# Eight bonus-sum products moved behind the last head's transposes, and their copy moved between two steps of the block inverses

## The reference

```python
def even_mixer(h, positions, w_in, ...):
    proj = h @ w_in
    a_qkv, b_rkv = proj[..., :3 * WIDTH_A], proj[..., 3 * WIDTH_A:]
    ...
    y_a = dilated_attention(q, k, v).transpose(0, 2, 1, 3).reshape(Bb, S, WIDTH_A)
    y_b = rwkv7_mixer(h, b_rkv, ...)
    return jnp.concatenate([y_a, y_b], axis=-1) @ w_out

def rwkv7_mixer(h, rkv, ...):
    ...
    ys = rwkv7_bidir_scan(both(r_h, 1), orient(heads(decay), 1), orient(k_dir, 1), orient(a_vec, 1), orient(b_vec, 1), both(v_h, 1))
    yf = unorient(ys, 1)
    ...
    bonus = (jnp.sum(r_h * (k_dir[0] + k_dir[1]) * r_k, axis=-1, keepdims=True) * v_h).reshape(Bb, S, WIDTH_B)
    return ((yn + bonus) * gate).astype(h.dtype)
```

## Time and profile before

| what | us |
|---|---|
| median of 3 runs | 1690.72 |
| lowest and highest of them | 1690.38, 1691.57 |
| time of the profiled execution | 1692.2 |
| its span, first to last instruction | 1690.5 |
| PE busy | 1655.8 |
| DVE busy | 1250.9 |
| ACT busy | 988.1 |
| POOL busy | 76.2 |

### The profile page before, as it was taken

One profiled execution on the slowest core, in us unless ns is written; L12 is line 12 of the kernel. 1 busy time (PEld: TensorE's weight loads), 2 busy tenths in 40 slices (PEclk: granted clock), 3 DMA queues, 4 the chain that ended last, 5 costly groups with the idle time before them and its releaser, 6 DMA issues.

```text
span 1690.5 us, 22416 instructions
## 1 busy us (share of the span) xinstructions
PE 1655.8 (98%) x8628; PEld 1370.1 (81%) x8628; DVE 1250.9 (74%) x1197; ACT 988.1 (58%) x958; POOL 76.2 (5%) x95
## 2 busy tenths in 40 slices
PE   7999999999999999899999999999999999999997
PEld 3868995999988885788888888888888888888886
DVE  5578545544423763788988888988888988988886
ACT  2356434443443432677677676776776777777774
POOL 2005230000000030000000000000000000000000
PEclk9999999999999999899999999999999999999999
DMA  6410014555542302899999999999999999999993
GB/s 244 110 70 27 2 51 150 175 177 198 174 150 100 133 18 102 303 368 378 325 366 374 330 366 370 330 365 368 334 364 367 329 366 353 350 366 351 345 378 123
DMA packets 199507, 428.86 MB, mean 254 GB/s; under 512 B 10746, under 2 KB 34574, under 8 KB 199438
## 3 DMA queue, kind: packets, MB, share of 16 engines
q1 hardware_dynamic: 199438, 427.90, 70.2%
HBM read 426.82 MB, written 1.05 MB: 253 GB/s over the span
## 4 chain that ended last, share of the span: by engine, by line
PE 97%; DVE 2%; ACT 1%; DMA 0%; issue 0%; SPq 0%; DVEq 0%; ACTq 0%
PE bank L2677 18%; PE bank L2679 18%; PE bank L2678 18%; PE bank L2457 5%; PE bank L2387 4%; PE bank L2388 4%; PE bank L2386 4%; PE bank L1962 2%; PE bank L1975 2%; PE bank L2152 2%; PE bank L2686 2%; PE bank L2620 2%; PE bank L2356 2%; PE bank L2175 2%; PE bank L2724 1%; PE bank L2538 1%
## 5 line engine op out<-in xcount | busy, mean ns | idle before, releaser
L1900 DVE TENSOR_TENSOR split<-ring,split 128x2048 fp32r<-128x2048 f32 x336 | 764.1, 2290 | 112.8 <-ACT split L1119 109.8
L1119 ACT ACTIVATE split<-ring 128x2048 fp32r<-128x2048 f32 x336 | 640.1, 1924 | 175.4 <-PE bank L2679 173.8
L2677 PE MATMUL bank<-split 128*128 128x512 f32 x896 | 354.6, 396 | 2.7 <-DVE split L1872 1.4
L2679 PE MATMUL bank<-split 128*128 128x512 f32 x896 | 349.8, 390 | 0.0
L2678 PE MATMUL bank<-split 128*128 128x512 f32 x896 | 349.1, 390 | 0.0
L2677 PEld LDWEIGHTS bank<-split 128*128 128x128 f32 x896 | 168.4, 188 | 36.2 <-issue 1.7
L2679 PEld LDWEIGHTS bank<-split 128*128 128x128 f32 x896 | 168.2, 188 | 35.8
L2678 PEld LDWEIGHTS bank<-split 128*128 128x128 f32 x896 | 168.6, 188 | 33.5
L2677 PE MATMUL bank<-split,ehr_ 128*128 128x512 f32 x448 | 180.6, 403 | 1.8 <-DVE ehr_ L1892 1.8
L2679 PE MATMUL bank<-split,ehr_ 128*128 128x512 f32 x448 | 175.6, 392 | 0.0
L2678 PE MATMUL bank<-split,ehr_ 128*128 128x512 f32 x448 | 175.3, 391 | 0.0
(11 more groups left out here) (478 smaller groups left out, 1972.7 us busy)
## 6 DMA issues: line engine op xcount, KB each, us to landing
ring<-in_od_moe_gate SPq DMA_DIRECT2D x112, 1024.0 KB, 6.9
ring<-in_od_moe_up SPq DMA_DIRECT2D x112, 1024.0 KB, 7.3
ring<-in_od_moe_down SPq DMA_DIRECT2D x112, 1024.0 KB, 6.5
ring<-in_od_w_in SPq DMA_DIRECT2D x7, 2048.0 KB, 7.6
ring<-in_ev_w_in SPq DMA_DIRECT2D x6, 2048.0 KB, 9.1
ring<-in_ev_ffn_gate SPq DMA_DIRECT2D x11, 1024.0 KB, 5.3
ring<-in_ev_ffn_up SPq DMA_DIRECT2D x11, 1024.0 KB, 7.9
ring<-in_ev_ffn_down SPq DMA_DIRECT2D x5, 2048.0 KB, 7.8
```

What stands on the lines that cost most here:

```text
L1119: act.activation(wst[:, r % NSTAGE, 0, :], ring[:, (r % NHALF) * HALF:(r % NHALF + 1) * HALF], ACT.Copy).then_inc(w_hi, 1)
L1900: dve.tensor_tensor(wst[:, r % NSTAGE, 1, :], ring[:, (r % NHALF) * HALF:(r % NHALF + 1) * HALF], wst[:, r % NSTAGE, 0, :].bitcast(F32), S ...
L2677: pe.matmul(o, hi, wh, start=start, stop=False)
L2679: return pe.matmul(o, lo, wh, start=False, stop=stop)
```

## The change

The products of token tile 0 stay where they were, behind the transposes of head 6. Those of token tile 1 are issued one step later, behind the transposes of head 7 and ahead of `values(7)`; the count `bon_ps` is raised by the last of them. `bonus_copy` is called inside level 8, behind its first `products`, and no longer ahead of the level.

```diff
@@ block_inverses
                     if b in meanwhile:
                         meanwhile[b]()
                     products(((Bk, b, w), 1, 32), ((Tb, 0, w), 32, 1))
+                    if (b, "products") in meanwhile:
+                        meanwhile[b, "products"]()
                     link(dve.tensor_reduce(strided(Xs, 0, (1, n * b * b)), strided(tmp, 0, (b, n * b * b), (1, b)),
                                            AX.X, ADD))
@@ vector
-            block_inverses(gather_all, {4: lambda: head_scores(7), 8: bonus_copy}, whole(Xm), Tb, whole(Tm), Xs, Tc, Pc).then_inc(dve_step, 1)
+            block_inverses(gather_all, {4: lambda: head_scores(7), (8, "products"): bonus_copy}, whole(Xm), Tb, whole(Tm), Xs, Tc, Pc).then_inc(dve_step, 1)
@@ tensor
-            def bonus_sums():
+            def bonus_sums(a):
                 pe.wait_ge(vt_sb, 2)
                 pe.wait_ge(dve_step, DVE_STEPS["bon_rdy"])
-                for a in range(TT):
-                    for j in range(4):
-                        last = pe.matmul(B[6][:, HA * a:HA * a + HA], bonT[:, SEQ * j + P * a:SEQ * j + P * a + P],
-                                         head_ind[:, j, :], start=(j == 0), stop=(j == 3))
-                last.then_inc(bon_ps, 1)
+                for j in range(4):
+                    last = pe.matmul(B[6][:, HA * a:HA * a + HA], bonT[:, SEQ * j + P * a:SEQ * j + P * a + P],
+                                     head_ind[:, j, :], start=(j == 0), stop=(j == 3))
+                if a == TT - 1:
+                    last.then_inc(bon_ps, 1)
@@
-                elif h == 6:
-                    bonus_sums()
+                elif h >= 6:
+                    bonus_sums(h - 6)
```

## The result

| kernel | runs | lowest | median | highest | above 1695 us |
|---|---|---|---|---|---|
| before | 22 | 1688.28 | 1691.53 | 1694.44 | 0 |
| changed | 22 | 1687.36 | 1706.51 | 1711.10 | 15 |

What follows compares the result with a forecast made beforehand. TensorE, busy in 98% of the span, was taken to bound the kernel. Filling its wait gains 0.45 us, VectorE's 0.2 delay stays under cover, so 1690.72 becomes 1690.3; range 1689.2 to 1691.7.

Steps and rivals of the forecast that it cites:

- The term of TensorE's list: Moved products fill TensorE's wait for ScalarE ahead of `values(7)`, which starts 0.42 to 0.97 us earlier by the clock; 0.45 taken.
- B: Rival, chance 0.25: the clock does not fall at 146, or later and more briefly; VectorE's cover limits the time to 1690.1.
- A: Forecast case, chance 0.45: the wait ahead of `values(7)` is filled, the clock's fall at 146.3 stays; 1690.3 us.
- The terms of VectorE and GpSimd: Level 8: copy costs 0; masks now meet VectorE's second pair of products, expansions 0.2 us later, between 1.0 earlier and 1.3 later.
- VectorE's cover lets only 0.65 through: 1690.1: At the inverse's second level, VectorE's 0.87 us of cover less its 0.2 delay lets at most 0.65 of TensorE's gain pass.
- The sign that the text gave for D: A wait of TensorE for VectorE between 157 and 163 us would show that the slower case held.
- D: Rival, chance 0.15: masks collide fully with VectorE's second pair of products, TensorE's second level begins 0.45 later; 1691.2 us.
- No case comes near that: the whole stretch touched, 143.67 to 158.94, is 15 us, and its largest term 2.0: Claimed no case reaches the 0.2%, 3.4 us, that a measurement can tell from no change; chance within 0.2% 0.94.
- A further fall of the clock ... could outweigh all of it: Caveat for elsewhere in the kernel: another fall, half as long (3.4 us), would cost 1.7 us in full work.
- The spread of the runs: Runs shown of the kernel before lay from 0.34 below to 0.85 above their median; the range was widened by these.

Runs made afterwards that it cites:

- e6: Changed kernel with GpSimd's first two masks held back until VectorE's second pair of products has ended: median 1689.68 us, 4 of 12 runs above 1695, ratio to before 1.0011.
- e2: Kernel before with only the VectorE half of the change (the moved copy): median 1692.84 us, 0 of 11 runs above 1695, ratio to before 1.0008.
- e9: Kernel before plus one useless 512-column product on TensorE behind the last head's transposes: median 1691.05 us, 0 of 12 runs above 1695, ratio to before 0.9999.
- e3: Changed kernel with useless products filling TensorE's gaps ahead of the first `level_x` and second `level_pt`: median 1692.84 us, 0 of 12 above 1695, ratio to before 1.0007.
- e4: Kernel before with three of level 8's last products done again on VectorE, making it late: median 1706.22 us, 6 of 8 above 1695, ratio to before 1.0086.
- e8: Changed kernel, gaps left empty, with three useless 512-column products ahead of the inverse's second level: median 1699.94 us, 6 of 6 above 1695, ratio to before 1.0052.
- e1: Changed kernel with its TensorE half alone, the copy back ahead of level 8: median 1703.23 us, 6 of 6 runs above 1695, ratio to before 1.0083.
- e5: Changed kernel with only the gap ahead of the first `level_x` filled by useless products: median 1691.03 us, 2 of 12 above 1695, ratio to before 1.0004.
- e10: Kernel before plus one useless 512-column product behind the last head's transposes, GpSimd's first two masks held back: median 1690.20 us, 0 of 12 above 1695, ratio 0.9991.

## Why the prediction was wrong

**The term of TensorE's list was right, for the case that I took as a rival.** The clock did not fall at 146 in the profiled execution, so B's numbers apply: `values(7)` at 146.82 (worked out: 146.73), `score(0)` at 147.82 (147.67). The forecast, A, took the old fall to stay, at 0.45 against 0.25; that was its first miss. B in turn priced the old fall up to `score(0)` alone, at 2.0. The half clock cost another 1.2 us between there and the inverse: TensorE was ready for `level_x` at 155.9 instead of 158.9, 3.0 earlier, and so ran into VectorE's first expansion, which had looked 2.0 away.

**The terms of VectorE and GpSimd were right.** Masks at 148.75 (148.69), the first pair 2.00 (2.0), the second pair's end at 153.07 (153.1), the pair of masks 3.37 (less than 3.93), the expansions 0.21 later (0.2). The masks' collision costs VectorE 1.25 (e6), and the change moved it from one pair to the other, nothing more (e2).

**The step that failed is "VectorE's cover lets only 0.65 through: 1690.1".** That TensorE would run into VectorE's expansions was seen, and the wait was priced at its own length, with the clock behind it put at nothing. While the clock holds, that price is about right: in e9's profile the second level starts at 161.76 against 162.49, 0.73 earlier. But the wait stands ahead of 26 us of products that are mostly 64 columns wide, and 15 of the 22 runs lie above 1695 with it. In the profiled one the clock fell for these products, 2.7 us behind the wait, and the stretch took 16.8 us more, the second gap included. e3 and e4 show it from both sides: filling the gaps takes the slow group away (0 of 12), making them in the kernel before brings it (6 of 8). The sign that the text gave for D, a wait of TensorE for VectorE between 157 and 163, did come; D's price for it, 1691.2, missed the clock in the same way. With it fell "No case comes near that: the whole stretch touched, 143.67 to 158.94, is 15 us, and its largest term 2.0". The stretch touched reached to 194.

**"A further fall of the clock ... could outweigh all of it" was in the text, with a price of 1.7.** That price took a fall half as long as the one in the earlier trace rows. The old fall lasted 6.8 us, with `score(0)` behind it (256 and 128 columns); that this work is why it was short fits e8 and is not shown by itself. The new one is followed by the inverse, and lasts 17 us in the profile of e1 and 34 in that of the changed kernel, though 3.4 in that of e5. The range allowed 1.7 for a fall; this one cost 15 net of all that was gained ahead of it.

**The spread of the runs was read wrongly.** Three runs within 1.2 us looked like a kernel whose time is settled. The 22 runs of before span 6.2 us, wider than the whole stated range of 2.5.

What stays open: why a gap of one length brings the fall in some executions and not in others (6 of 8 in e4, 15 of 22 in the changed kernel), why the fall lasts 3.4, 17 or 34 us in the same work, and why e9 has no run above 1695 where e6 has four. Whether real work could stand in the two gaps in place of the useless products was not tried.

## What to carry to other kernels

A wait on TensorE costs its own length plus what the clock does behind it. Before closing one wait, look at which engine TensorE will meet next, and at what kind of work follows: with three dense products behind it the fall was 6.8 us long (e8), with a long run of narrow ones up to 34. Making TensorE earlier without making the engine that it meets earlier by as much only moves the gap, here to the worst place in the kernel. And a kernel whose time hangs on such a fall has to be judged by the list of its runs: three runs can all come from one group.

## What the runs showed of the hardware

A clock at 0.50 can stand for 34 us with TensorE busy: between 165 and 194 its busy share was 100%, and the engine ran float32 products of 64 columns for the most part, with some of 128, each with a 128-column weight load. At 1.00 the same work keeps its clock (the 25.83 us stretch of before). How long the low level lasts in it differs from one execution to the next, 3.4 us (e5), 17 (e1) or 34. With three products of 512 columns in between it was back after 6.8 (e8).

The clock does not fall in the gap but behind it: 1.8 us (e5), 1.9 (e1), 2.4 (e8) and 2.7 (changed kernel) after TensorE had started again. And a gap is not needed: the fall at 146.3 of the kernel before came with TensorE 100% busy from 142 on, 1.0 us behind the end of its 16 eight-column products. e9 and e10 have the same 16 products and no such fall, so these do not always bring it.

The Trainium skill (TensorE: Matmul & The Clock Gate, A second HAM failure mode: psum-queue depth-cycling) tells of a kernel in which small and frequent idle times between groups of matmuls make the clock swing. The traces agree that small ones can be enough, here without being frequent: a fall followed one gap of 1.27 us (changed kernel), one of 1.69 (e1) and one of 0.82 (e5). They add that the way back can fail for tens of microseconds without any further gap.

The two idle times did not weigh the same: with the first filled 2 of 12 runs lay above 1695, with the first cut to 0.20 and the second at 0.82, 4 of 12, with both filled none. With 0.43 and 0.81, in the kernel before, none of 12 did either (e9).
